# A hybrid attention and pooling step on one core: gate rows broadcast through memory, the turn to the output projection reordered, and the probabilities' transposes moved inside projection units

## The reference, cut to what matters

```
mod = silu(c) @ w_ada + b_ada;  shift, scale, gate = split(mod, 3)
h = layer_norm(x) * (1 + scale) + shift
q, k, v, g_attn, u, g_pool = split(h @ w_in)          # 2304 columns
o_attn = sink_attention(rope(q), rope(k), v)          # chunks of 64, own chunk and two before
o_pool = (trailing mean of u over 2, 4, 8 or 16 rows - u) @ w_pool * pool_scale
mixed = concat(o_attn * silu(g_attn), o_pool * silu(g_pool))
r = 2**0.25 * x + gate * (mixed @ w_out)
y = layer_norm(r) * ln_g + ln_b
```

## Time and profile before

| what | value |
|---|---|
| median of 3 runs | 454.52 us (452.95 to 456.77) |
| the profiled execution | 454.26 us, span 452.5 us |
| TensorE matmuls busy | 430.8 us (95%) |
| VectorE, ScalarE, GpSimd busy | 269.9, 126.5, 131.0 us |
| mean granted TensorE clock | 0.991 of full speed |

### The profile page before, as it was taken

How to read it: one execution, slowest core, us unless ns; L and a number is a source line. 1 busy time by engine, 2 the same in 40 slices (tenths; PEclk the granted TensorE clock), 3 DMA queues, 4 the chain that set the end, 5 groups by cost and what they waited for, 6 DMA issues and landing times.

```text
span 452.5 us, 6743 instructions
## 1 busy us (share of the span) xinstructions
PE 430.8 (95%) x2612; PEld 369.4 (82%) x2612; DVE 269.9 (60%) x534; ACT 126.5 (28%) x309; POOL 131.0 (29%) x102
## 2 busy tenths in 40 slices
PE   5699989999999999999999999999998999999993
PEld 2358978989999998879879988898956778888883
DVE  6536793411146676355774664676646887888875
ACT  3355532221110003344333433432463100000000
POOL 2546542201222220562234032222052333333300
PEclk9999999999999999999999999999999999999997
DMA  8999400607113210110101010120614022222231
GB/s 298 416 420 391 205 1 1 234 0 291 46 49 121 65 46 7 46 33 24 53 8 48 5 48 8 46 54 3 191 36 151 1 93 94 93 93 94 93 129 58
DMA packets 22545, 46.30 MB, mean 102 GB/s; under 512 B 11089, under 2 KB 13649, under 8 KB 21202
## 3 DMA queue, kind: packets, MB, share of 16 engines
q1 hardware_dynamic: 22514, 45.88, 28.6%
HBM read 40.61 MB, written 6.17 MB: 103 GB/s over the span
## 4 chain that ended last, share of the span: by engine, by line
PE 83%; DVE 8%; ACT 4%; issue 2%; DMA 2%; SPq 1%; POOL 1%; DVEq 0%; ACTq 0%
PE proj_ps L645 13%; PE proj_ps L647 13%; PE proj_ps L646 13%; PE proj_ps L781 8%; PE proj_ps L783 7%; PE proj_ps L782 7%; PE s_ps L539 2%; PE s_ps L681 2%; PE t_ps L710 2%; DMA wada<-w_ada 2%; PE proj_ps L608 2%; PE proj_ps L595 2%; ACT Pb L948 1%; PE t_ps L568 1%; PE proj_ps L596 1%
## 5 line engine op out<-in xcount | busy, mean ns | idle before, releaser
L645 PE MATMUL proj_ps<-h_hi,w_hi 128*128 128x384 f32 x384 | 132.9, 346 | 0.0
L647 PE MATMUL proj_ps<-h_hi,w_lo 128*128 128x384 f32 x384 | 129.1, 336 | 0.0
L646 PE MATMUL proj_ps<-h_lo,w_hi 128*128 128x384 f32 x384 | 129.1, 336 | 0.0
L1322 POOL TENSOR_TENSOR w_lo<-w_raw,w_hi 128x1024 fp32r<-128x1024 f32 x16 | 41.3, 2579 | 157.3 <-ACT w_hi L894 157.3
L645 PEld LDWEIGHTS proj_ps<-h_hi,w_hi 128*128 128x128 f32 x384 | 72.2, 188 | 4.2 <-issue 2.2
L646 PEld LDWEIGHTS proj_ps<-h_lo,w_hi 128*128 128x128 f32 x384 | 72.3, 188 | 0.9
L647 PEld LDWEIGHTS proj_ps<-h_hi,w_lo 128*128 128x128 f32 x384 | 72.2, 188 | 0.0
L781 PE MATMUL proj_ps<-wo_hi,m_hi 128*128 128x512 f32 (+1 forms) x152 | 58.6, 386 | 1.5 <-DVE mixed L1125 1.5
L783 PE MATMUL proj_ps<-wo_hi,m_lo 128*128 128x512 f32 (+1 forms) x152 | 58.4, 384 | 0.0
L782 PE MATMUL proj_ps<-wo_lo,m_hi 128*128 128x512 f32 (+1 forms) x152 | 58.4, 384 | 0.0
L1120 DVE SCALAR_TENSOR_TENSOR mixed<-th,proj_ps 128x384 f32<-128x384 f32 x24 | 13.3, 553 | 49.9 <-ACT th L908 49.9
(11 more groups left out here) (157 smaller groups left out, 611.6 us busy)
## 6 DMA issues: line engine op xcount, KB each, us to landing
w_raw<-w_in SPq DMA_DIRECT2D x18, 512.0 KB, 4.1
wada<-w_ada SPq DMA_DIRECT2D x8, 1024.0 KB, 17.4
xs<-x_all SPq DMA_DIRECT2D x9, 512.0 KB, 11.7
xf<-x_all SPq DMA_DIRECT2D x9, 512.0 KB, 4.1
wada_late<-w_ada SPq DMA_DIRECT2D x2, 2048.0 KB, 8.3
y_out<-yr SPq DMA_DIRECT2D x8, 512.0 KB, 2.9
wo_raw<-w_out SPq DMA_DIRECT2D x4, 512.0 KB, 3.3
wo_rest<-w_out SPq DMA_DIRECT2D x4, 512.0 KB, 8.8
```

Of the source, the lines that this page charges most:

```text
L645: pe.matmul(bank[:, 0:CW], w_hi[:, w, k, :], hi, start=(k == 0), stop=False)
L646: pe.matmul(bank[:, 0:CW], w_hi[:, w, k, :], lo, start=False, stop=False)
L647: mm = pe.matmul(bank[:, 0:CW], w_lo[:, w, k, :], hi, start=False, stop=(k == KT - 1))
L1322: pool.tensor_tensor(w_lo[:, b % 2], w_raw[:, b % RAW], w_hi[:, b % 2].bitcast(F32), ALU.subtract).then_inc(wlo_done, 1)
```

## The change

It has three parts.

*Gate rows through memory.* The four r units, `ebc` and the bias row in `part` are gone. After the last modulation part is evacuated, SP stores the four partial results (9 rows each) to memory (`g_parts`), loads them back as 128 partitions of 72 values beside the bias (`gq`), GpSimd adds them in three instructions behind its low part of block 8 (`gate_rows`), SP stores the sum (`g_rows`), and when the last pooling group no longer needs its buffers, nine broadcast loads fill `gateB`. VectorE waits for them ahead of its first gate product.

*Order of the turn.* z(0,0) follows gp(0,1) directly, and slot 18 stands behind z(0,0). VectorE makes pool_mean(0) ahead of the evacuation of gp(0,0). ScalarE makes mixed_high(0) and wo_high(3) behind z(0,0), ahead of slot 18. GpSimd takes wo_low(0) and wo_low(1) and the low part of tile 0 (`mixed_low(0)`); VectorE makes wo_low(2) behind gp(0,0), and wo_low(5), (6) and (7) behind the last unit, ahead of slot 19.

*Transposes inside units.* The transposes of step s-2 are made inside the unit before slot s, behind its slice 1 (`TRANSPOSED_IN`, `T_SLICE`). Slot s has the values of step s-3 and the scores of step s. The copies of the transposes of step s-2 stand in slot s of VectorE and ScalarE, and `mix` of step s-3. There is a slot more: slot 20 is behind output 1, 21 behind output 3 and 22 behind output 4; step 18's transposes are inside the pair of outputs 0 and 1, step 19's inside output 3.

```diff
+GROWS = 1 + NSEQ
+GQ = GROWS * D // P
         if s == 3:
-            units += [("r", row, half) for row in range(2) for half in range(2)]
             units.append(("z", g, 0))
-SLOTS = {PLACES[4 * s // 3]: [s] for s in range(NSTEP + 2)}
+SLOTS = {PLACES[4 * s // 3]: [s] for s in range(NSTEP + 3)}
+SLOTS[unit_index("z", GROUPS[3], 0)] = SLOTS.pop(unit_index("gp", GROUPS[3], 1))
+TRANSPOSED_IN = {max(m for m in range(n + 1) if block_of(m) is not None) if n < NU else n: s[0] - 2 for n, s in SLOTS.items() if 2 <= s[0] < NSTEP + 2}
+T_SLICE = 1
-POOL_WO = (3, 4)
+POOL_WO = (0, 1, 3, 4)
-WO_HIGH_AFTER = {unit_index("gp", GROUPS[3], 0): range(0, 3), unit_index("r", 1, 1): range(3, 6), LAST_PROJ: range(6, KT)}
-WO_LOW_AFTER = {unit_index("gp", GROUPS[3], 0): (0, 1, 2), unit_index("r", 1, 1): (5,), NU - 1: (6, 7)}
+WO_HIGH_AFTER = {unit_index("gp", GROUPS[3], 0): range(0, 3), unit_index("z", GROUPS[3], 0): range(4, 6), LAST_PROJ: range(6, KT)}
+WO_LOW_AFTER = {unit_index("gp", GROUPS[3], 0): (2,), NU - 1: (5, 6, 7)}
...
 SP
-            sp.dma_start(part[9:10, :, :], brow_d).then_inc(ld_brow, 16)
+            for g in range(4):
+                sp.dma_start(g_parts[g], part[32 * g:32 * g + GROWS, :, :]).then_inc(st_parts, 16)
             load_w(6)
             load_w(7)
             load_w(8)
+            sp.wait_ge(st_parts, 64)
+            sp.dma_start(gq[:, 0:4, :], g_parts.rearrange("g s a n -> g (s a n)").rearrange("g (p q) -> p g q", q=GQ)).then_inc(ld_parts, 16)
+            sp.dma_start(gq[:, 4, :], brow_d).then_inc(ld_parts, 16)
...
             load_w(12)
+            sp.wait_ge(gate_sum, 1)
+            sp.dma_start(g_rows.rearrange("s n -> (s n)").rearrange("(p q) -> p q", q=GQ), gq[:, 0, :]).then_inc(st_rows, 16)
...
             for k in range(RAW, KT):
                 load_w_out(k)
+            sp.wait_ge(d_done, 4)
+            sp.wait_ge(st_u, 32 * 4)
+            sp.wait_ge(st_rows, 16)
+            sp.dma_start(gateB[:, 0, :], g_rows[0:1, :].to_broadcast([P, D])).then_inc(ld_gate, 16)
+            for s in range(NSEQ):
+                sp.dma_start(gateB[LS * s:LS * (s + 1), 1, :], g_rows[1 + s:2 + s, :].to_broadcast([LS, D])).then_inc(ld_gate, 16)
...
 TensorE
                     for k in range(KT):
+                        if k == T_SLICE + 1 and n in TRANSPOSED_IN:
+                            p_transposes(TRANSPOSED_IN[n])
...
             def slot(i):
-                if 0 <= i - 2 < NSTEP:
-                    values(i - 2)
-                if 0 <= i - 1 < NSTEP:
-                    p_transposes(i - 1)
+                if 0 <= i - 3 < NSTEP:
+                    values(i - 3)
                 if i < NSTEP:
                     scores(i)
...
                 output((0, 1), k)
+                if k == T_SLICE and NU + 1 in TRANSPOSED_IN:
+                    p_transposes(TRANSPOSED_IN[NU + 1])
...
                     output((m,), k)
+                    if k == T_SLICE and NU + m in TRANSPOSED_IN:
+                        p_transposes(TRANSPOSED_IN[NU + m])
...
 ScalarE
+                if UNITS[n] == ("z", GROUPS[3], 0):
+                    mixed_high(0)
+                    wo_high(3)
                 for i in SLOTS.get(n, []):
                     slot(i)
...
 VectorE (mix, and the copies to PT2 and PT3, one slot later; ScalarE's copy to PT1 likewise)
+                if UNITS[n] == ("gp", GROUPS[3], 0):
+                    pool_mean(j)
                 evac_unit(n)
-                if UNITS[n] == ("z", GROUPS[3], 0):
-                    dve.wait_ge(mhi_done, 1)
-                    dve.tensor_tensor(m_lo[:, 0], mixed[:, :, 0:P], m_hi[:, 0].bitcast(F32), ALU.subtract).then_inc(mlo_v, 1)
...
-                    dve.wait_ge(act_free, freed_count(unit_index("r", 1, 1))[1])
+                    dve.wait_ge(ld_gate, 16 * GROWS)
...
 GpSimd
+            def gate_rows():
+                pool.wait_ge(ld_parts, 32)
+                link(pool.tensor_tensor(gq[:, 0:2, :], gq[:, 0:2, :], gq[:, 2:4, :], ALU.add))
+                link(pool.tensor_tensor(gq[:, 0, :], gq[:, 0, :], gq[:, 1, :], ALU.add))
+                pool.tensor_tensor(gq[:, 0, :], gq[:, 0, :], gq[:, 4, :], ALU.add).then_inc(gate_sum, 1)
...
                 w_low(b)
+                if b == 8:
+                    gate_rows()
...
+            wo_low(0)
+            wo_low(1)
+            mixed_low(0)
+            wo_low(3)
+            wo_low(4)
```

More of the change, by code:

```diff
@@ L278, in hybrid_step @@
     m_lo = place("m_lo", [P, 2, KT, P], F32R, at=r_hl + 2 * KT * P * 4)
+    r_part = top[0]
     part = place("part", [P, 2, 512])
+    gq = place("gq", [P, 5, GQ], at=r_part)
     wp = place("wp", [P, 4, P])
@@ L631, in unit @@
                     pe.wait_ge(d_done, GROUPS.index(j) + 1)
-                    pe.wait_ge(ld_small, 80)
+                    pe.wait_ge(ld_small, 64)
                     dd = sB if j % 2 == 0 else sA
                     mm = pe.matmul(bank[:, 0:CW], wp[:, j, :], dd[:, cols(c)], start=True, stop=True)
-                elif kind == "r":
-                    pe.wait_ge(ld_brow, 16)
-                    mm = pe.matmul(bank[:], ebc[:, j, :], part[:, c, :], start=True, stop=True)
                 else:
@@ L1166, in slot @@
             def slot(i):
-                if 0 <= i - 2 < NSTEP:
-                    mix(i - 2)
-                if 0 <= i - 1 < NSTEP and keys_of(i - 1)[1]:
-                    k2 = keys_of(i - 1)[1]
-                    w = 512 if i - 1 < NQ else 256
-                    if i - 1 >= NQ:
+                if 0 <= i - 3 < NSTEP:
+                    mix(i - 3)
+                if 0 <= i - 2 < NSTEP and keys_of(i - 2)[1]:
+                    k2 = keys_of(i - 2)[1]
+                    w = 512 if i - 2 < NQ else 256
+                    if i - 2 >= NQ:
                         k2 = P
-                    dve.wait_ge(t_done, i)
-                    if i >= 2:
-                        dve.wait_ge(pv_done, i - 1)
-                    if packed(i - 1):
+                    dve.wait_ge(t_done, i - 1)
+                    if i >= 3:
+                        dve.wait_ge(pv_done, i - 2)
+                    if packed(i - 2):
                         dve.tensor_copy(PT2[0:QB, 0:256], t_ps[0:QB, 1, 0:256])
@@ L1382, in _, with wo_low, mixed_low @@
             window_sums(3, 1)
-            for k in POOL_WO:
+            def wo_low(k):
                 pool.wait_ge(whi_done, NBLK + k + 1)
                 pool.tensor_tensor(wo_lo[:, k, :], w_out_raw(k), wo_hi[:, k, :].bitcast(F32), ALU.subtract).then_inc(wlo_done, 1)
+            def mixed_low(t):
+                pool.wait_ge(mhi_done, t + 1)
+                pool.tensor_tensor(m_lo[:, t % 2], mixed[:, :, P * t:P * (t + 1)], m_hi[:, t % 2].bitcast(F32), ALU.subtract).then_inc(mlo_p, 1)
+            wo_low(0)
[3 more added lines that the diff above has]
+            wo_low(4)
             for t in range(TILES):
                 if t + 1 < TILES:
-                    pool.wait_ge(mhi_done, t + 2)
-                    pool.tensor_tensor(m_lo[:, (t + 1) % 2], mixed[:, :, P * (t + 1):P * (t + 2)], m_hi[:, (t + 1) % 2].bitcast(F32),
-                                       ALU.subtract).then_inc(mlo_p, 1)
+                    mixed_low(t + 1)
                 inv_std(TILES + t)
@@ L1433, in tables @@
             sel[32 * g + s, s] = 1.0
-        ebc[32 * g, 0, :] = 1.0
-        for s in range(NSEQ):
-            ebc[32 * g + 1 + s, 1, LS * s:LS * (s + 1)] = 1.0
-    ebc[9, :, :] = 1.0
-    return cos, np.ascontiguousarray(sin), ident, sel, ebc
+    return cos, np.ascontiguousarray(sin), ident, sel
 def kernel(x_prompt, x_sample, cache_k, cache_v, state_pool, c_prompt, c_sample, w_ada, b_ada, w_in, attn_sinks, w_pool,
```

48 lines of the change are left out of this document (20 added, 28 removed).

## The result

The changed kernel takes 453.49 us (median of 20 runs, 450.56 to 454.76); the kernel before, 20 runs on the same chips, 455.41 (452.86 to 458.38). The ratio is 0.9955, 95% interval 0.9935 to 0.9974: 2.05 us less by that ratio (0.45%; 1.92 between the two medians), which is real but within 1%. Forecast were 450.8 and a gain of 3.5.

What follows compares the result with a forecast made beforehand. TensorE's own queue was taken as the bound, its matmuls busy 430.8 of 452.5 us. Savings less late-copy waits and an extra slot (+0.25) summed to -3.55; from 454.26 that gave 450.8 us, range 446.5 to 455.5.

Steps and rivals of the forecast that it cites:

- part 4: Turn reordered: output products could start 9.6 us after gp(0,1) ends, where it was 16.4; four copies queued badly.
- The 1.5 us idle goes: At the turn, TensorE's idle before the first output product disappears: -1.5 us.
- GpSimd's extra copies ... are hidden: At the turn, GpSimd's added copies, some 2.4 to 3.3 us each, cost nothing; low part due 5 us before use.
- Gate units out, 4.6; broadcasts at 0: Before the output, eight matmul records and their wait leave TensorE: -4.6 us; the gate rows' broadcast loads cost 0.
- 0.12 a step: Transposes moved from slots into units save this much in each of 20 steps: -2.4 us (0 to -3.2).
- Waits for Pb gone, no wait in adjacent pairs, +0.9 in unit 45: Normalised-probability waits go, -1.2 us; five adjacent pairs have margin 0.7; behind pool_mean, slot 10's late copy adds 0.9.
- Late copies, +0.7, +1.3, +1.7 and +1.6: TensorE waits for transpose copies in the last unit, first output pair, output 3 and behind output 4, in us.
- main forecast: Whole kernel at 450.8 us, 448.8 to 452.6, chance 0.55.
- longer waits: Rival: GpSimd-stretched VectorE operations eat the 0.7 margin in five adjacent pairs, each up to 0.6: +3, 453.8 us; chance 0.15.
- The copies did not come in time: Rival claimed the opposite: the last four copy waits, 5.3 us, are absent, giving 445.5 us; chance 0.18.
- The insertion itself did not stall: Rival claimed a stall at 20 points inside units, 0.35 us each: +7, 457.8 us; chance 0.09.
- The broadcasts were on time: Rival claimed gate rows come late and the first tile waits: 456 us or more; chance 0.03.

Runs made afterwards that it cites:

- C: Changed kernel with GpSimd waiting for step 18's normalised probabilities before wo_low(3): 453.97 us, ratio 0.9967 to the kernel before.
- M: Changed kernel with GpSimd's mixed_low(0), wo_low(3) and wo_low(4) each cut into four instructions, order and start kept: 452.50 us, ratio 0.9921 to the kernel before.
- A: Changed kernel with the transposes put back into the slots, gate rows and turn order kept: 450.09 us, ratio 0.9880 to the kernel before.
- B: Changed kernel with VectorE's slots 20, 21 and 22 moved between a tile's statistics and its normalisation: 448.60 us, ratio 0.9853 to the kernel before.
- D: Changed kernel with VectorE's slot 19 moved ahead of wo_low(5) to (7): 453.36 us, ratio 0.9943 to the kernel before.
- E: Changed kernel with ScalarE's copy of step 16's transposes moved ahead of mixed_high(0) and wo_high(3): 451.45 us, ratio 0.9919 to the kernel before.
- F: Changed kernel with VectorE's product and copies of slot 10 moved ahead of pool_mean(2): 452.24 us, ratio 0.9927 to the kernel before.
- I: Changed kernel with transposes back in the slots and GpSimd waiting for step 18's probabilities before wo_low(3): 448.67 us, ratio 0.9834 to the kernel before.
- G: Changed kernel, five edits: tail slots before normalisation, wo_low(3) delayed, slot 19 before wo_low(5), ScalarE's slot 18 copy first, slot 10 copies before mean: 445.93 us.
- J: Changed kernel with GpSimd waiting for step 18's probabilities before wo_low(3) and VectorE's slot 19 ahead of wo_low(5) to (7): 451.42 us, ratio 0.9901.

## Why the prediction was wrong in size and right in kind

**The step that failed** is the sentence in part 4, "The 1.5 us idle goes", with "GpSimd's extra copies ... are hidden". The wait before the first output product was still 1.38 us. I asked of GpSimd's added work only whether TensorE waits for its results, and not what it holds on VectorE meanwhile. C and M show the cause: without a subtraction beside them (two of the three in C), or with short ones (M), VectorE's operations shrink and that wait is gone. The profile of before had the hint, which I used in part 4 for the tail alone: 3.30 against 1.28 us for one operation. The Trainium skill, SBUF — State Buffer, Who interferes with whom, says that of a VectorE operation with two SBUF inputs and a GpSimd operation that reads SBUF the later to issue blocks fully until the first is through; the ends of the six rows above agree within 0.32 us. By that rule, with the durations of these rows, each small operation on VectorE's path beside a GpSimd subtraction was to be priced at up to 2.4 us.

The forecast sum was -3.55. With 1.38 of idle that stayed it is -2.17; measured were -2.13 between the traces and -2.05 by the runs' ratio. Of the miss of 2.7 us in the time itself another 1.15 lies in the base: 454.26, the profiled execution's time, while the median of 20 runs of before is 455.41.

**By its steps:**
1. *Gate units out, 4.6; broadcasts at 0*: as forecast. A, which differs from before by this and the turn, starts its output 4.38 sooner; with the 1.92 that it waits for step 18's probabilities that is 6.3, where 4.6 + 1.5 + 0.3 were forecast.
2. *0.12 a step*: measured 0.13. The sum by the rule of the Trainium skill, TensorEngine Tiling (Array Packing), Key Properties, that a change of tiling mode drains TensorE, was -3.2, 0.16 a step, and was not reached: 0.10 of gap is left between values and scores, and six transposes cost 0.67 inside a unit.
3. *Waits for Pb gone, no wait in adjacent pairs, +0.9 in unit 45*: measured 0.85, and no other.
4. *Late copies, +0.7, +1.3, +1.7 and +1.6*: 0.73 (0.9 with the rest of that gap), 1.26, 1.61 and 1.62. The 1.26 is right in part by luck. Its 0.3 for a GpSimd subtraction beside the first split did not occur: GpSimd ends at 333.82 and the first split begins at 335.58. But the splits, late by the same held operations, began behind the output's start (335.50) and not 0.4 ahead of it. B, D and E, and F for the 0.85, show for each that it is queue order: with the copy moved forward in the queue, that wait is gone.

**The rivals.** 453.49 lies outside the main forecast's 448.8 to 452.6 and inside the 452.6 to 455.5 that "longer waits" had at 0.15. The copies did not come in time. The insertion itself did not stall: at the 16 places where the copy was in time the list of waits has nothing. "A part of the waits is longer", by VectorE operations that GpSimd stretches, had the right mechanism and the wrong place, five pairs of adjacent units where GpSimd happens not to be in the way; at 3 us for all five it was too vague to be priced where it struck. The broadcasts were on time.

What is shown: that the insertion as queued cost 2.26 us net in the traces. With its copies in time it is worth 3.2 to 3.8 between the traces of I and G, and 2.2 by the runs, where 0 is at the edge of the interval. Not shown: which of G's five edits could be left out.

## What to carry to other kernels

When work is moved to GpSimd, list the VectorE operations with two SBUF inputs that will begin beside it, and price each at the rest of the GpSimd instruction in hand; a two-number operation on the critical chain can cost 2.4 us. Keep GpSimd away from that stretch, or cut its instructions into pieces. When a step is delayed by a stage to free one engine, walk every other engine's queue for what now stands ahead of its copies: here some 7 us were freed up to the output (8.3 less the work that only moved), and 4.5 of it came back in three waits for late copies that two reorderings (B and D) removed. And mend such waits together: C and D by themselves moved the wait to the next place and gave nothing clear of noise, all five gave 7.7.

## What the runs showed of the hardware that I had not expected

- **A VectorE operation is held, not slowed.** Two numbers a row took 2.22 or 2.31 us beside a GpSimd subtraction of 2.4, 0.58 beside one in quarters, 0.16 alone, and 0.16 when it began 0.12 us ahead of GpSimd (E). It goes the other way too: in the changed kernel GpSimd's m_lo subtraction of 353.47 starts beside VectorE's L1310 (352.91 to 354.22, two inputs in SBUF) and takes 3.00 us in place of 2.39; VectorE's next operation of the kind, L1313, starts at 354.25 and takes 3.31. The one that comes second is held each time.
- **TensorE's clock can fall behind a wait of some 2 us.** In C behind 2.81 us of idle and in D behind 2.02, the granted clock went to 0.50, the lower level, some 0.8 to 1.4 us after work had resumed, and stayed there for 3.4 us: 1.5 us lost each time. Behind 2.53 (J), 2.02 (M), 1.95 (E) and 1.92 us (A) it did not. D and M have the same 2.02, so the length of the idle alone does not decide it in these runs; what does stays open. I had priced every wait at its own length.
- **The first 40 us differ from run to run**: in the traces of the changed kernel's variants, the same products up to there were granted 0.85 to 1.00 of full speed in the first 20 us and 0.81 to 1.00 in the next, and step 0's scores start between 168.84 (A) and 173.24 us (D). Spans of single executions can't be compared for an effect of 2 us; parts counted from a common point behind the start could.
